# The gate put on the identity two picks ahead of the dot product, in a layer of pooling, gated DeltaNet and product-key experts

## What is computed

```python
top_s, top_pos = lax.top_k(cand_s, PEER_TOPK)
gates = jax.nn.softmax(top_s.astype(jnp.float32), axis=-1).reshape(T, PEER_HEADS * PEER_TOPK)
u = expert_u[experts]
act = jax.nn.gelu(jnp.einsum('td,tkd->tk', h_t, u).astype(jnp.float32), approximate=False)
vv = expert_v[experts]
return jnp.einsum('tk,tkd->td', (gates * act).astype(h_t.dtype), vv).astype(h_t.dtype)
```

## Time and profile before

| what | value |
|---|---|
| median of 3 runs | 3116.89 us (3116.49 to 3123.21) |
| the profiled execution | 3123.21 us |
| its span | 3121.4 us |
| mean granted clock of TensorE | 0.876 of full speed |
| busy: TensorE, VectorE, ScalarE, GpSimd | 74%, 70%, 48%, 39% |
| DMA, mean over the span | 370 GB/s |
| picks: first gather issued, last | 344.3 us, 3091.5 us |

### The profile page before, as it was taken

How to read it: one execution, slowest core, us unless ns; L and a number is a source line. 1 busy time by engine, 2 the same in 40 slices (tenths; PEclk the granted TensorE clock), 3 DMA queues, 4 the chain that set the end, 5 groups by cost and what they waited for, 6 DMA issues and landing times.

```text
span 3121.4 us, 39271 instructions
## 1 busy us (share of the span) xinstructions
PE 2303.5 (74%) x13004; PEld 1081.1 (35%) x13004; DVE 2199.2 (70%) x5450; ACT 1506.3 (48%) x4168; POOL 1232.4 (39%) x1168
## 2 busy tenths in 40 slices
PE   8988687867787678866877677767786677765665
PEld 4447344423443244323433233323332233321211
DVE  1453687777777788778777777767777788776664
ACT  3433255655554455655554444544544444444443
POOL 1000343444444444443444444444444444444442
PEclk9999888988889888988899888988888889988777
DMA  3254599999999999999999999999999999999997
GB/s 121 78 188 142 227 384 376 405 411 389 406 387 411 418 403 372 401 414 408 385 389 411 399 413 394 402 421 398 409 400 412 399 416 414 402 408 421 421 421 329
DMA packets 192682, 1155.17 MB, mean 370 GB/s; under 512 B 20576, under 2 KB 48352, under 8 KB 60896
## 3 DMA queue, kind: packets, MB, share of 16 engines
q0 software_dynamic: 147456, 1073.81, 84.1%
q1 hardware_dynamic: 30560, 56.85, 5.2%
q10 hardware_dynamic: 14464, 22.02, 1.9%
HBM read 1136.61 MB, written 15.99 MB: 369 GB/s over the span
## 4 chain that ended last, share of the span: by engine, by line
DMA 37%; PE 29%; DVE 12%; ACT 7%; issue 4%; POOL 3%; POOLq 0%; ACTq 0%; DVEq 0%
DMA ring_mem<-in_experts,work 37%; PE bank L1503 15%; DVE ring_mem L1259 6%; PE bank L1451 3%; POOL ring_mem L721 3%; PE bank L1466 3%; PE bank L1291 3%; ACT work L956 1%; ACT work L952 1%; PE bank L1429 1%; PE bank L1385 1%; ACT work L950 1%; ACT L950 1%; ACT L863 1%; PE bank L1504 1%
## 5 line engine op out<-in xcount | busy, mean ns | idle before, releaser
L721 POOL DMA_INDIRECT ring_mem<-in_experts,work x1024 | 1160.7, 1134 | 1525.2 <-PE bank L1504 1330.4
L1259 DVE CUSTOM_DVE_ANT_0 ring_mem<-ring_mem,work 128x1024 f32<-128x1024 f32 x1024 | 1253.6, 1224 | 576.4 <-DMA ring_mem<-in_experts,work 566.7
L1503 PE MATMUL bank<-ring_mem,work 64*64 64x512 f32 x4096 | 1227.5, 726 | 552.6 <-ACT work L956 545.6
L1504 PE MATMUL bank<-ring_mem,work 64*64 64x512 f32 x4096 | 1227.7, 726 | 0.0
L950 ACT ACTIVATE work<-work 128x1 f32<-128x1 f32 x1024 | 206.5, 202 | 1204.7 <-DVE work L1259 1167.5
L1503 PEld LDWEIGHTS bank<-ring_mem,work 64*64 64x64 f32 x4096 | 294.1, 153 | 1212.2 <-ACT work L956 738.2
L956 ACT ACTIVATE work<-kept,work 128x64 f32<-128x64 f32 x1024 | 357.3, 349 | 33.5
L952 ACT ACTIVATE work<-work 128x1 f32<-128x1 f32 x1024 | 301.8, 295 | 33.3
L1291 PE MATMUL bank<-work 128*128 128x128 f32 x1080 | 195.0, 322 | 138.9 <-ACT work L818 73.9
L1504 PEld LDWEIGHTS bank<-ring_mem,work 64*64 64x64 f32 x4096 | 292.9, 153 | 0.0
L1291 PEld LDWEIGHTS bank<-work 128*128 128x128 f32 x1080 | 160.1, 219 | 275.8 <-ACT work L818 96.2
(11 more groups left out here) (269 smaller groups left out, 2234.0 us busy)
## 6 DMA issues: line engine op xcount, KB each, us to landing
ring_mem<-in_experts,work POOLq DMA_INDIRECT x1024
ring_mem<-in_wc ACTq DMA_DIRECT2D x31, 512.0 KB
ring_mem<-in_w_query SPq DMA_DIRECT2D x16, 576.0 KB, 4.1
late<-in_wc SPq DMA_DIRECT2D x16, 512.0 KB, 3.5
work<-kept_tiles SPq DMA_DIRECT2D x42, 128.0 KB
x_all<-in_w_out SPq DMA_DIRECT2D x1, 4096.0 KB, 13.8
work<-in_x SPq DMA_DIRECT2D x8, 512.0 KB
out<-work SPq DMA_DIRECT2D x8, 512.0 KB
```

The costliest lines, as they stand in the source:

```text
L721: G.indirect_dma_start(ring[slot(g)], None, a["experts"], bass.IndirectOffsetOnAxis(ap=pick_now[:, k:k + 1], axis=0)).then_inc(got[slot(g) ...
L1259: V.tensor_tensor_reduce(out=row, in0=row, in1=hf_tile[t % 2], scale=1.0, scalar=0.0, op0=ALU.mult, op1=ALU.add, accum_out=dots[:, k:k + 1 ...
L1503: PE.matmul(low_sum[half][high if odd else low], of[low], row[low], start=(q == 1), stop=(q == PICKS - 1))
L1504: m = PE.matmul(high_sum[half][low if odd else high], of[high], row[high], start=(q == 1), stop=(q == PICKS - 1))
```

## The change

The gate no longer multiplies the gelu's column. A new function of ScalarE, `gated_identity(q)`, multiplies the identity by the gate of pick q and puts it into pick q's diagonal buffer. It is called for picks 0 and 1 ahead of the loop and then at the end of each `pick` for the pick two further on. `pick` itself makes the gelu and multiplies the buffer by it in place. The buffer `weights` is gone; the semaphore `weights_made` now counts gated identities. The wait for `gates_scaled` and the wait for the diagonal buffer's last matmuls (`used`) are in the new function. The number of waits of a pick stays the same.

```diff
--- before.py
+++ after.py
@@ -585,7 +585,7 @@
         same = cut(2 * TOPK * TOPK)
         left, pairs = same[:, 0:2 * P], same[:, 2 * P:4 * P]
         pos, pos_hl = cut(TOPK).bitcast(U32), found.bitcast(U32)
-        dots, scored_gelu, weights = cut(TOPK), cut(TOPK), cut(TOPK)
+        dots, scored_gelu = cut(TOPK), cut(TOPK)
         state = cut(HEADS * P)
         f_stat, n_stat = stat[:, 0:4], stat[:, 4:8]
         ring = [ring_mem[:, n * 2 * DM:(n + 1) * 2 * DM] for n in range(RING)]
@@ -942,18 +942,23 @@
                         act.dma_start(to.rearrange("t p k -> p t k"),
                                       unit_now[:, 0:PW].rearrange("p (t k) -> p t k", t=PASS)).then_inc(U["stored"], 16)

+                def gated_identity(q):
+
+                    j, k = q % PICKS // TOPK, q % TOPK
+                    if k == 0:
+                        act.wait_ge(X["gates_scaled"], q // TOPK + 1)
+                    act.wait_ge(X["used"], USED0 + q + 1 - DIAGS)
+                    A.activation(diag[k % DIAGS], pair_ident, ACT.Copy, scale=gates[:, ds(j * TOPK + k, 1)]).then_inc(X["weights_made"], 1)
+
                 def pick(t, j, k):
                     n = t * PICKS + j * TOPK + (k + 1)
-                    if k == 0:
-                        act.wait_ge(X["gates_scaled"], t * PHEADS + j + 1)
                     act.wait_ge(X["dot_made"], n)
                     A.activation(scored_gelu[:, k:k + 1], dots[:, k:k + 1], ACT.Gelu).then_inc(X["gelu_made"], 1)
                     act.wait_ge(X["gelu_made"], n)
-                    A.activation(weights[:, k:k + 1], scored_gelu[:, k:k + 1], ACT.Copy,
-                                 scale=gates[:, ds(j * TOPK + k, 1)]).then_inc(X["weights_made"], 1)
                     act.wait_ge(X["weights_made"], n)
-                    act.wait_ge(X["used"], USED0 + n - DIAGS)
-                    A.activation(diag[k % DIAGS], pair_ident, ACT.Copy, scale=weights[:, k:k + 1]).then_inc(X["diag_made"], 1)
+                    A.activation(diag[k % DIAGS], diag[k % DIAGS], ACT.Copy, scale=scored_gelu[:, k:k + 1]).then_inc(X["diag_made"], 1)
+                    if n + 1 < TILES * PICKS:
+                        gated_identity(n + 1)

                 for s in range(STEPS):
                     delta(s, 0)
@@ -966,6 +971,8 @@
                 next_root(0)
                 turned(0)
                 gate(0, 0)
+                gated_identity(0)
+                gated_identity(1)
                 for t in range(TILES):
                     last = t == TILES - 1
                     for q in range(PICKS):
```

## The result

| kernel | median of the runs | ratio to before (95% interval) | granted clock | span of the profiled execution |
|---|---|---|---|---|
| before | 3117.2 us | 1 | 0.876 | 3121.4 us |
| after | 3101.0 us | 0.9948 (0.993 to 0.9967) | 0.878 | 3107.2 us |
| after, a second time | 3101.7 us | 0.996 (0.9941 to 0.9978) | 0.876 | 3098.3 us |

The change made the kernel faster by 12 to 16 us, 0.4 to 0.5%. The forecast was 3113.2 us and no change that can be told; the measured median lies 1 us under the range, near the 15 us of rival (a).

A forecast was written before the change was run, and what follows sets the result against it. The prediction took the DMA transfers' rate as the bound. Dip savings of 1.6, 1.2, 0 and 0.6 us plus 0.32 for the tail, together 3.7, brought the median from 3116.9 to 3113.2 us; range 3102 to 3123.

The forecast's parts named there:

- rival (a): Gather queue: dips come in runs, so a lap's saving carries into the next; 15 us, 3102, taken at 3106; chance 0.21.
- The bound: DMA engines, 380 to 3095 us: transfers set the rate, so shortening wins at most the dips' 43 to 55 us.
- The dips, once each: 24 separate dips in DMA share, each gaining at most 0.32 us; 3.7 us together, bounds 0.5 and 7.7.
- Five tile-start dips: Dips in DMA share at the start of a tile: each takes the whole 0.32 us, 1.6 us together.
- the eight: Dips hanging on a DeltaNet or gate step of ScalarE behind a pick: 0.15 us each, 1.2 us together.
- three signs of being wrong: Dips' sum falling over 8 us, full stretches above 421 GB/s, or mean granted clock below 0.87 with growing dips.
- The steps behind a pick: ScalarE's instructions following a diagonal, with their DMA issues: 0.06 us earlier, 0.76 us after gelu's start instead of 0.82.
- The moved waits: ScalarE's waits for the buffer's last matmul and the scaled gates, now in a pick's tail: cost nothing.
- The in-place copy: ScalarE's diagonal with input and output the same buffer: taken at 349 ns, like the copy between two buffers.
- rival (d): ScalarE: the in-place copy, with two waits ahead of it, starts later and eats the gain; 3116.9 us; chance 0.03.
- (b): Ring of gathers: transfers are not at their roof and each lap counts; some 34 us gained, 3083; chance 0.03.
- (c): TensorE: six more pairs on laps of dips run at half clock, 10 us lost, less 3.7 won; 3123.4; chance 0.13.

The follow-up runs named there:

- single picks: The kernel after with TensorE taking each pick by itself, not two at a time, so the even pick's slot is released earlier: 3068.2 us, ratio 0.9849.
- the square: Ratios of four kernels: before (1), before without the weight product (0.9907), after (0.9948 and 0.996), after with one more one-column copy between gelu and diagonal (1.0024).
- The two copies: The kernel after with two more one-column copies in series between gelu and diagonal: 3162.5 us, ratio 1.0141.
- the copies on 55% of the picks: The kernel after with two extra copies between gelu and diagonal only for picks 13 to 82 of each tile, 560 of 1024: 3146.3 us, ratio 1.0101.

## Why the prediction was wrong

**The bound.** "Those 43 to 55 us are all that any shortening could win": this step failed. It took the DMA share of 0.99 for the used part of the transfers' rate. The share counts a packet that takes longer as busy. The rate says more: 404 GB/s over the stage against 422 in the full 50 us at 3000 is 4% of 2715 us, by this estimate some 115 us of room, part of it taken up by smaller transfers that run beside the gathers. No run went past 55 us: single picks took 44 us over the kernel before on the same chip, 53.7 between the traces' stretches. But 23.7 of these came out of the packets' own time, which no sum of dips holds, and shortfalls of 28.5 us still stood in its 5 us stretches up to 3040 us. So 43 to 55 was not a bound.

**The dips, once each.** "Five tile-start dips take the whole 0.32 ... the eight take 0.06": the sum of 3.7 us was the term of wrong size. The 0.32 us was right (0.33 measured), but in the square the way is worth 22 to 29 us, 7 to 9% of the 328 us that 1024 picks lose, not 1%, and the whole change 12 to 16. The 5 us stretches under 0.90 went from 29 with 42.8 us to 26 with 35.5 (up to 3080 us, before the last landing), 7 us, about half of the gain. All shortfalls from a share of 1 together fell from 55 to 47 us, so most of the other half does not stand in the DMA share at all. The upper end of the sum, 24 x 0.32 = 7.7, was no bound either, for the same reason. The two copies showed the slope directly. None of the three signs of being wrong that the prediction named came: the dips' sum fell by less than 8 us, the full 50 us near the end stood at 421 GB/s in after, and the clock at 0.878.

**The steps behind a pick.** "Come 0.06 us earlier": measured 0.10. But I priced these steps only on eight dips and only by the difference, and took the effect as small. Left out or in, that copy moves the time by 7 to 15 us.

**ScalarE's busy time** "up by 55": down by 58.6, since the view counts overlap once. The rows that I had read, 0.26 us from start to start of 0.35 us copies, held the answer.

**The moved waits** at nothing: right. **The in-place copy** at 349 ns: right; rival (d) fell. **The rivals**: (a) gave 15 us, close to what was measured, by a mechanism (laps in a row) that was only near it; the copies on 55% of the picks show that sensitivity is wider than the dips. (b) had the right view, that a lap's saving is felt outside of dips, at twice the size; I argued it away by the share of 1.01 in the last 300 us. There the queue is full: of the last 128 gathers of before 8 began with at most two issued, of each 128 in the first half 44 to 57. (c) did not come: in after the clock stayed at 0.878. What a higher clock alone would do stays open, since it came to 0.97 only together with twice the steps, and that brought nothing. The Trainium skill's limit of 358 GB/s for a core (DMA: Bandwidth & Descriptors, Specifications), by which the sum would have been 0, did not bind: up to 416 GB/s over 1250 us with single picks. The Trainium skill's same page (DMA: Bandwidth & Descriptors, Measured) gives about 358 GB/s as what each of the two cores of an HBM domain gets while both stream; the prediction took it for the roof of a core alone. This kernel runs on one core; no run here used two. The ceiling of 435 in the first table of the Trainium skill's page (DMA: Bandwidth & Descriptors, Specifications) was not reached: the full 50 us of before stood at 422 GB/s.

## What to carry to other kernels

A DMA share near 1 does not say that the transfers run at their rate: set the GB/s of the stage against the GB/s of a stretch in which the queue is surely full, and the difference is the room. In a ring, price a step between landing and release by what a slot's time is worth (here 50 to 90 us for a microsecond on all 1024 picks), by a run that adds a copy or takes a slot away, not by counting dips. Releasing a slot as early as its data is used (33 us here) was worth twice the shortening of the chain (12 to 16 us).

## What was not expected of the hardware

- A granted TensorE clock of 0.97 in place of 0.88, which came with twice the steps for a pair of picks, left the time where it was (3107.8 against 3101 us).
- Two 128x64 ScalarE copies of 349 and 333 ns, started 0.26 us apart, fill the engine less than a serial pair of 295 and 349 ns: 58.6 us less busy time over 1024 picks.
- One ring slot of eight, over 464 picks, is worth 30 us (412 to 401 GB/s).
